# Splitting the last weight panels of two attention cores by columns instead of by contraction halves

## The reference

```python
def chunk_attention(u, w_in, b_in, rel_bias, w_out):
    q, k, v = jnp.split(u @ w_in + b_in, 3, axis=-1)
    ...
    s = jnp.einsum('bhtd,bhjd->bhtj', qi, kb).astype(jnp.float32) + bias
    p = jax.nn.softmax(jnp.where(mb, s, NEG_INF), axis=-1).astype(vb.dtype)
    return jnp.einsum('bhtj,bhjd->bhtd', p, vb)

def odd_mixer(h, w_in, b_f, qnorm_g, knorm_g, w_out):
    q, k, v, g, fl = jnp.split(proj, ...)
```

## Time and profile before

| what | value |
|---|---|
| median of 3 runs | 1955.74 us |
| the profiled execution's own time | 1954.02 us |
| its span | 1952.3 us |
| TensorE busy | 1828.4 us, 94% |
| VectorE / ScalarE / POOL busy | 1202.0 / 754.5 / 799.3 us |
| mean granted TensorE clock | 0.964 |
| first attention core, from its first scores | 756.1 to 917.6 us |
| second attention core | 1740.9 to 1904.1 us |

### The profile page before, as it was taken

How to read it: one execution, slowest core, us unless ns; L and a number is a source line. 1 busy time by engine, 2 the same in 40 slices (tenths; PEclk the granted TensorE clock), 3 DMA queues, 4 the chain that set the end, 5 groups by cost and what they waited for, 6 DMA issues and landing times.

```text
span 1952.3 us, 24973 instructions
## 1 busy us (share of the span) xinstructions
PE 1828.4 (94%) x9107; PEld 1475.1 (76%) x9107; DVE 1202.0 (62%) x1783; ACT 754.5 (39%) x1180; POOL 799.3 (41%) x577
## 2 busy tenths in 40 slices
PE   4997999999999999989999999998999999999989
PEld 3775687788888777767778888886788777777767
DVE  5786456976677942654587777687388733125562
ACT  3333335222222333544432222325335545554450
POOL 4432335556556443222446556552423343432222
PEclk8998999999999999988999999998999999999899
DMA  8543325455554232221266455541211222322211
GB/s 329 194 151 114 124 87 183 151 159 178 175 170 146 93 114 85 68 73 66 65 200 203 154 172 164 172 140 52 78 65 59 77 67 68 105 89 74 66 55 44
DMA packets 116905, 235.70 MB, mean 121 GB/s; under 512 B 8113, under 2 KB 25393, under 8 KB 115793
## 3 DMA queue, kind: packets, MB, share of 16 engines
q1 hardware_dynamic: 113776, 227.17, 35.5%
q10 hardware_dynamic: 3040, 7.34, 1.1%
HBM read 232.36 MB, written 2.13 MB: 120 GB/s over the span
## 4 chain that ended last, share of the span: by engine, by line
PE 40%; issue 34%; POOL 20%; DVE 4%; ACT 2%; POOLq 0%; DVEq 0%; ACTq 0%
PE bank L216 20%; POOL wsp L2189 19%; PE bank L429 9%; PE bank L1272 2%; PE bank L1313 2%; PE bank L1276 1%; PE bank L1383 1%; PE bank L1367 1%; PE bank L1344 1%; PE bank L1771 1%; PE bank L1548 1%; ACT wsp L179 0%; PE bank L313 0%; PE bank L619 0%; DVE fP L1445 0%
## 5 line engine op out<-in xcount | busy, mean ns | idle before, releaser
L2189 POOL TENSOR_TENSOR wsp<-raw,wsp 128x512 fp32r<-128x512 f32 x528 | 786.3, 1520 | 1133.0 <-ACT wsp L179 1133.0
L216 PE MATMUL bank<-xT,wsp 128*128 128x512 f32 x2592 | 606.9, 394 | 5.2 <-POOL wsp L2189 3.6
L216 PEld LDWEIGHTS bank<-xT,wsp 128*128 128x128 f32 x2592 | 487.7, 189 | 116.0 <-issue 7.5
L179 ACT ACTIVATE wsp<-raw 128x2048 fp32r<-128x2048 f32 x132 | 252.0, 1913 | 576.1 <-PE bank L429 248.4
L429 PE MATMUL bank<-wsp,hT 128*128 128x512 f32 x1344 | 322.0, 400 | 10.4 <-POOL wsp L2189 8.3
L216 PE MATMUL bank<-wsp,xT 128*128 128x512 f32 x1248 | 305.1, 400 | 17.7 <-DVE gg L1148 9.8
L429 PEld LDWEIGHTS bank<-wsp,hT 128*128 128x128 f32 x1344 | 255.5, 191 | 74.9 <-issue 9.0
L216 PEld LDWEIGHTS bank<-wsp,xT 128*128 128x128 f32 x1248 | 234.8, 191 | 75.5 <-DVE gg L1148 10.5
L530 DVE TENSOR_TENSOR h<-h 128x512 f32<-128x512 f32 x64 | 57.2, 909 | 79.9 <-ACT h L487 79.6
L547 DVE TENSOR_TENSOR htmp<-bank,gate 128x512 f32<-128x512 f32 x112 | 76.8, 686 | 47.8 <-PE bank L429 47.8
L1272 PE MATMUL bank<-xT,wsp 128*128 128x512 f32 x384 | 100.2, 411 | 0.3 <-DVE gT L1688 0.3
(11 more groups left out here) (304 smaller groups left out, 2133.8 us busy)
## 6 DMA issues: line engine op xcount, KB each, us to landing
raw<-in_ff_w SPq DMA_DIRECT2D x64, 1024.0 KB, 5.5
ada_ring<-in_w_ada SPq DMA_DIRECT2D x48, 384.0 KB, 3.6
ada_ring<-in_ada_w SPq DMA_DIRECT2D x48, 384.0 KB, 3.7
ring<-in_w_ada SPq DMA_DIRECT2D x64, 256.0 KB, 3.2
raw<-in_odd_w_in SPq DMA_DIRECT2D x16, 1024.0 KB, 5.5
raw<-in_gla_w_in SPq DMA_DIRECT2D x12, 1024.0 KB, 5.9
raw<-in_att_w_in SPq DMA_DIRECT2D x12, 1024.0 KB, 5.1
raw<-in_even_w_in SPq DMA_DIRECT2D x12, 1024.0 KB, 5.1
```

Source lines behind the costliest of these rows:

```text
L179: act.activation(wsp[:, slot, 0], raw[:, slot], ACT.Copy).then_inc(hi_made, 1)
L216: mm = pe.matmul(out_ap, l, r, start=(start and n == 0), stop=(stop and n == 2))
L2189: ins = pool.tensor_tensor(wsp[:, slot, 1, k], raw[:, slot, k], wsp[:, slot, 0, k].bitcast(F32), ALU.subtract)
```

## The change

The three panels inside each core become six column halves: 256 columns over the whole contraction, 1 MB each, half number `half` in slot `half % 2`. `by_columns` views a slot as 8 k tiles of 256 columns. `sp_column_half` loads one, in runs of 256 floats. A column half holds two T tiles of 128 rows of the result, or four N tiles of 256 columns. A T tile is cut along k into pieces of 4 + 4 (`TWO`), 3 + 3 + 2 (`THREE`) or 2 + 2 + 2 + 2 k (`FOUR`), one for each unit; an N tile stays in one unit. The units are consecutive: the first core has pieces in units 0 to 26, the second in 0 to 31. In the second core the values, four tiles of 512 columns before, become eight of 256. The last tile of a half releases one slot; the iteration's eviction comes ahead of that slot's copy. The order of columns, of `bank_free` numbers and of gate tiles follows (in the second core: gates 0 to 3, values of pairs 4 and 5, gates 4 and 5, values of pairs 6 and 7, gates 6 and 7). SP's order around it is the same, with six loads for six in each core.

```diff
-                tiles += 22 if n == "att_in" else 3 * c
+                tiles += 3 * PHASE0[n] + 10 if n in PHASE0 else 3 * c
...
+        def by_columns(half):
+            return half.rearrange("p k (two n) -> p (k two) n", two=2)
+        def sp_column_half(sp, name, half, at):
+            j = base[name] + 2 * PHASE0[name] + half
+            sp.wait_ge(lo_made, j - 1)
+            sp.dma_start(by_columns(raw[:, half % 2]), W[name][:, :, at:at + COLS // 2]).then_inc(raw_ld[half % 2], 16)
...
+        def in_slots(halves):
+            out, u, n, done = {}, 0, 0, 0
+            for half, tiles in enumerate(halves):
+                for i, (kind, at, cuts) in enumerate(tiles):
                     last = i == len(tiles) - 1
-                    if tile[0] == "N" and tile[3] == COLS // 2:
-                        out[u] = [(seq, i, k, tile, 0, last), (seq, i, k, tile, 1, last)]
+                    done += not last
+                    for k0, k1 in zip((0, *cuts), (*cuts, KT)):
+                        out[u] = (half, i, n, kind, at, k0, k1, last, done)
                         u += 1
+                    n += 1
...
+        TWO, THREE, FOUR = (4,), (3, 6), (2, 4, 6)
+        def turned_tiles(p, *cuts):
+            return [("T", (p, i), c) for i, c in enumerate(cuts)]
+        VALUES = [("N", t, ()) for t in range(ST)]
+        ATT_IN = in_slots([turned_tiles(4, THREE, TWO), turned_tiles(5, THREE, TWO), VALUES,
+                           turned_tiles(6, THREE, TWO), turned_tiles(7, TWO, TWO), VALUES])
+        ODD_IN = in_slots([turned_tiles(0, THREE, THREE), turned_tiles(2, TWO, THREE), VALUES,
+                           turned_tiles(4, THREE, TWO), VALUES, turned_tiles(6, FOUR, FOUR)])
...
+        def gate_number(p):
+            return p if p < 4 else p + 4 if p < 6 else p + 8
...
+        def wait_slot_tile(eng, name, piece):
+            half, last, done = piece[0], piece[7], piece[8]
+            if last:
+                eng.wait_ge(w_used, base[name] + 2 * PHASE0[name] + half + 1)
+            else:
+                eng.wait_ge(tile_done, tile0[name] + 3 * PHASE0[name] + done)
...
+        def pe_slot_piece(pe, name, ts, piece):
+            half, i, number, kind, _, k0, k1, last, _ = piece
+            if k0 == 0:
+                pe.wait_ge(TS[ts]["bank_free"], KT + ST * PHASE0[name] + number)
+            for k in range(k0, k1):
+                if i == 0 and k % 2 == 0:
+                    low_ready(pe, base[name] + 2 * PHASE0[name] + half, k // 2)
+                for n, (a, b) in enumerate(PASSES):
+                    start, stop = k == 0 and n == 0, k == KT - 1 and n == 2
+                    w = by_columns(wsp[:, half % 2, b])[:, k]
+                    if kind == "T":
+                        mm = pe.matmul(bank[D_BANK][:, :], w[:, i * P:i * P + P], xT[:, a, k, :], start=start, stop=stop)
...
-        T4 = [("T", i) for i in range(4)]
-        ATT_IN = in_slots([(0, 3, T4), (10, 4, [("T", 0), ("T", 1)] + [("N", t, COLS // 2, COLS // 2) for t in range(ST)]),
-                           (20, 5, [("T", 0), ("T", 1)] + [("N", t, COLS // 2, COLS // 2) for t in range(ST)])])
-        ODD_IN = in_slots([(0, 5, T4), (10, 6, [("N", t, 0, COLS) for t in range(ST)]), (20, 7, T4)])
...
-        def wait_slot_tile(eng, name, seq, i, last):
-            if last:
-                eng.wait_ge(w_used, base[name] + 2 * seq + 2)
-            else:
-                eng.wait_ge(tile_done, panel_tile(name, seq, i))
...
+                        mm = pe.matmul(bank[D_BANK][:, 0:COLS // 2], xT[:, a, k, i * P:i * P + P], w, start=start, stop=stop)
+            if k1 == KT:
+                mm.then_inc(w_used if last else tile_done, 1)
...
-                for piece in work.get(u, []):
-                    pe_slot_piece(pe, name, ts, piece)
+                if u in work:
+                    pe_slot_piece(pe, name, ts, work[u])
...
-            if name == "att_in":
-                before = 6 if p < 6 else 12
-            else:
-                before = 4
+            before = 4 if p < 6 else {"att_in": 12, "odd_in": 10}[name]
...
-                for seq, i, k, tile, h, last in now:
+                if u in work and work[u][6] == KT:
+                    half, _, _, kind, at, _, _, last, _ = work[u]
+                    wait_slot_tile(act, name, work[u])
+                    evac(half, kind, at)
                     if last:
-                        act_high(act, base[name] // 2 + seq + 1, h)
-                for seq, i, k, tile, h, last in now:
-                    if h == 1:
-                        wait_slot_tile(act, name, seq, i, last)
-                        evac(seq, i, tile)
+                        act_high(act, base[name] // 2 + PHASE0[name] + half // 2 + 1, half % 2)
...
+            def evac(half, kind, at):
+                if kind == "T":
+                    p, i = at
+                    (query, key)[i](p, bank[D_BANK][:, :]).then_inc(free, 1)
                 else:
-                    c = COLS + (seq - 4) * (COLS // 2)
-                    act.activation(tok[:, tile[1], c:c + COLS // 2], bank[D_BANK][:, 0:COLS // 2], ACT.Copy).then_inc(free, 1)
+                    c = COLS if half == 2 else COLS + COLS // 2
+                    act.activation(tok[:, at, c:c + COLS // 2], bank[D_BANK][:, 0:COLS // 2], ACT.Copy).then_inc(free, 1)
...
-            tile_of = {4: (0, 1), 5: (2, 3), 6: (4, 5), 7: (10, 11)}
+            tile_of = {4: (0, 1), 5: (2, 3), 6: (8, 9), 7: (10, 11)}
...
+            def evac(half, kind, at):
+                if kind == "N":
+                    c = COLS if half == 2 else COLS + COLS // 2
+                    act.activation(tok[:, at, c:c + COLS // 2], bank[D_BANK][:, 0:COLS // 2], ACT.Copy).then_inc(free, 1)
                 else:
-                    if seq == 7:
-                        act.wait_ge(s["ol"], PAIRS + i + 1)
-                    act.activation(gT[:, i], bank[D_BANK][:, :], ACT.Tanh, scale=0.5).then_inc(s["z"], 1)
+                    p = sum(at)
+                    if p >= ST:
+                        act.wait_ge(s["ol"], PAIRS + p - ST + 1)
+                    act.activation(gT[:, p % ST], bank[D_BANK][:, :], ACT.Tanh, scale=0.5).then_inc(s["z"], 1)
...
+                if u in ODD_IN and ODD_IN[u][3] == "T" and ODD_IN[u][6] == KT:
+                    p = sum(ODD_IN[u][4])
+                    dve.wait_ge(s["z"], p + 2)
+                    dve.scalar_tensor_tensor(gT[:, p % ST], gT[:, p % ST], 1.0, bank[D_BANK][:, :], ALU.add, ALU.mult)\
+                        .then_inc(free, 1)
...
-                    dve.wait_ge(free, KT + 5 * ST + (p + 1 if p < ST else ST + p + 1))
+                    dve.wait_ge(free, KT + 5 * ST + gate_number(p) + 1)
...
-            sp_panels(sp, "att_in", 6)
+            sp_panels(sp, "att_in", PHASE0["att_in"])
+            for half in range(6):
+                sp_column_half(sp, "att_in", half, PHASE0["att_in"] * COLS + half * (COLS // 2))
             sp_panels(sp, "att_out", 2)
...
-            for seq, panel in enumerate((0, 2, 1, 3, 4, 6, 5, 7)):
+            for seq, panel in enumerate((0, 2, 1, 3, 4)):
                 for h in range(2):
                     sp_half(sp, base["odd_in"] + 2 * seq + h, h, W["odd_in"][:, HK * h:HK * h + HK, panel * COLS:panel * COLS + COLS])
                 if seq == 3:
                     fox_sp_bias(sp)
+            for half, panel in enumerate((6, 6.5, 5, 7, 5.5, 7.5)):
+                sp_column_half(sp, "odd_in", half, int(panel * COLS))
             sp_panels(sp, "odd_out", 2)
...
-    order = [q[0:4], k[0:4], v[0:4], q[4], k[4], q[5], k[5], q[6], k[6], v[4:6], q[7], k[7], v[6:8]]
+    order = [q[0:4], k[0:4], v[0:4], q[4], k[4], q[5], k[5], v[4:6], q[6], k[6], q[7], k[7], v[6:8]]
```

More of the change, by code:

```diff
@@ new lines, in in_slots @@
+            return out
+        TWO, THREE, FOUR = (4,), (3, 6), (2, 4, 6)
[6 more added lines that the diff above has]
+                           turned_tiles(4, THREE, TWO), VALUES, turned_tiles(6, FOUR, FOUR)])
@@ L1398, in act_pairs @@
             for u in range(NU + 4):
-                now = work.get(u, [])
                 if u >= 6 and u % ST == high_at:
@@ L1632, in fox_act @@
             act.preload_act_table_set("exp_and_others")
-            def evac(seq, i, tile):
-                if tile[0] == "N":
-                    act.activation(tok[:, tile[1], COLS:D], bank[D_BANK][:, :], ACT.Copy).then_inc(free, 1)
-                else:
-                    if seq == 7:
-                        act.wait_ge(s["ol"], PAIRS + i + 1)
-                    act.activation(gT[:, i], bank[D_BANK][:, :], ACT.Tanh, scale=0.5).then_inc(s["z"], 1)
+            def evac(half, kind, at):
+                if kind == "N":
+                    c = COLS if half == 2 else COLS + COLS // 2
+                    act.activation(tok[:, at, c:c + COLS // 2], bank[D_BANK][:, 0:COLS // 2], ACT.Copy).then_inc(free, 1)
+                else:
+                    p = sum(at)
+                    if p >= ST:
```

(8 more changed lines are left out.)

## The result

The changed kernel takes 1936.85 us (median of 4 runs, 1933.62 to 1939.97) against 1956.40 us for the kernel before beside it: ratio 0.9899, 95% interval 0.9883 to 0.9914, so 19.6 us less. The forecast was 1941.0 with a range of 1929 to 1951; the likeliest case, 1936 to 1947, holds it.

A forecast was written before the change was run, and what follows sets the result against it. TensorE, busy 94% of the span, left idle or low-clock time to win: holes 28.4 us, tails 16.9. Terms -28.4 + 0.9 + 1.6 + 15.2 + 1.0 - 5.1 = -14.8 us gave 1941.0, range 1929 to 1951.

The forecast's parts named there:

- the likeliest case: Whole kernel: the prediction's own forecast, 1936 to 1947 us, chance 0.55.
- Holes filled: Units without pieces in the middle of both cores: their 28.4 us go if new pieces are ready and hide as much.
- PE work: Second core's four 512-column value tiles become eight of 256: +0.9 us; first core 0.
- Loads and slot conversions: 1 KB load runs, landing in 5.1 to 21 us, and slots ready 7.2 us after their last tile: 0.
- rival D: Pieces not ready (1 KB runs, or slot copy queued behind exp), PE stands at low parts: 1956 to 1965; chance 0.04.
- Short pieces: Bare 2-k pieces at 512-wide units (7 first core, 27 and 31 second) cost about 0.5 us each: +1.6 us.
- VectorE against POOL: VectorE's scalings and splits delayed by POOL's low parts beside filled units: +15.2 us, bounds 0 and 40.
- the low clock behind such waits: Lower PE clock after long waits: 1.5 us at unit 15 of the first core, 1.5 at unit 11 of the second.
- Tails: Bare units at each core's end: first core +1.0 us, second core -5.1 us (3.5 lost instead of 8.6).
- A: Better: slack takes nearly all of the VectorE and POOL contention, 4 instead of 15.2: -26, 1930 us; chance 0.2.
- B: Small gain: contention costs 26, not 15.2: -3, so 1953 us (1948 to 1955); chance 0.15.
- C: Slower: VectorE's scaling and splits beside POOL's low parts cost more than 30 us; at 36, 1962 us; chance 0.06.

The follow-up runs named there:

- POOL's low parts thin: Changed kernel with low parts of the twelve slots converted inside the cores cut from 512 to 32 columns, the rest left out: 1928.2 us, ratio 0.9864.
- the dense runs: Two kernels with column halves and consecutive 4-k pieces, against the kernel before: units 0 to 23, 1934.3 us; units 3 to 26, 1952.6 us.
- the offset run: Column halves with consecutive 4-k pieces, every piece three units later (units 3 to 26 instead of 0 to 23): 1952.6 us, 0.9980 of the kernel before.
- dense 4-k kernel: Changed kernel with every 512-column tile in two 4-k pieces, consecutive in units 0 to 23 of both cores: 1934.3 us, 0.9891 of the kernel before.
- the kernel with holes kept: Column halves, but 4-k pieces only at the units where pieces stood before, so holes stay bare: 1948.4 us, 0.9965 of the kernel before.

## Why the prediction was right, and where its terms were off

Direction, range and likeliest case hold, and the mechanism is shown: PE had no piece in the holes, and the gain is where the holes were. The sum, -14.8 against -19.6 measured (-22.1 by the cores), is 5 to 7 us short. By its own steps, and with its own measure, from start to start: a wait in brackets is less than the time lost by it, since a piece without a wait behind it lasts some 0.16 us longer than it holds up the next row. (826.86 to 830.05 in the changed kernel, a 3-k piece in front of a wait of 0.85 us, is 3.19 instead of 2.19, so 1.00 lost.)

- **Holes filled, -28.4.** No wait over 1 us is left in units 8, 9, 18 and 19 of either core. Right.
- **PE work, +0.9.** Right as far as it went, but it left out that a cut costs something itself. Two pieces of the changed kernel, start to start, 763.65 to 765.84 in the first core for 3 k and 1753.53 to 1755.03 in the second for 2 k, give 2.19 and 1.50 us, so 5.88 for 3 + 3 + 2 against 5.72 for 4 + 4, and 6.0 for four pieces. Seven tiles of the one kind and two of the other: 1.7 us that were not in the sum.
- **Loads and slot conversions, 0.** 5.1 to 5.2 us to land, at the lower bound of 5.1 to 21. Inside the first core no matmul waits for a low part, in the second PE's only such wait is 0.2 us of a weight load. Right, and rival D is out.
- **Short pieces, +1.6.** The waits at 2-k pieces in front of 512-wide units are 0.32 (unit 7), 0.32 and 0.30 us, which is 0.48, 0.47 and 0.47 from start to start: the 0.5 each was right. But there are two that I had at nothing, 0.29 and 0.28 us (0.44 lost each) at the 2-k piece of unit 2 in either core, beside a 384-wide unit.
- **VectorE against POOL, +15.2.** The step that was mis-sized. All waits of PE beside pieces, this term and the one before together, are 3.1 us in the first core and 5.5 in the second by the brackets, 8.6; from start to start 4.1 and 7.3, so 11.4 against 16.8. With POOL's low parts thin, 0.9 and 2.3 of that are left, so VectorE against POOL is some 8 us. Where I had taken a conversion beside a 512-wide unit (15, 19, 23 in the first core; 15 in the second) there is a wait, 0.85, 0.85, 0.77 and 1.07 us (1.00, 1.02, 0.92 and 1.22 lost; I had 2.0, 0.65, 0.65 and 1.4 without the clock). The 3 us for the low clock behind such waits do not exist. The PE timeline of the second core at its worst wait, and the next:

```profile
1780.68 0.44 PE L1385 MATMUL bank<-fPT,tok 128*64 128x128 f32 x4 [0.59 <-DVE gT L1693]
...
1785.62 0.88 PE L1369 MATMUL bank<-ident,fP 128*128 128x128 f32 x6 [1.44 <-DVE fP L1442]
...
1806.75 0.87 PE L1369 MATMUL bank<-ident,fP 128*128 128x128 f32 x6 [1.07 <-DVE fP L1442]
```

  The VectorE operations that I named for unit 11 (gate product, output product, split) do stand in a row ahead of its reduces. They cost 0.59 us before its piece, which stays with POOL's low parts thin, and the scalings 1.44 behind it (0.65 and 1.60 lost), instead of 2.5 + 1.5; six transposes behind it take 0.88 us, the full clock. Units 5 and 6 of the first core, which I had at 1.2, show no wait (0.26 lost in unit 6), although VectorE is held up there by POOL's block of 780.98 to 786.76:

```profile
781.12 1.52 DVE L1324 CAST aqr<-aq 128x512 fp32r<-128x512 f32 x1
782.68 1.66 DVE L1325 TENSOR_TENSOR aqr<-aq,aqr 128x512 fp32r<-128x512 f32 x1
784.26 0.54 DVE L1434 CUSTOM_DVE_ANT_0 aP<-bank,abt 128x384 f32<-128x384 f32 x1
```

  The cast takes 0.42 alone and the subtraction 0.69, but the 3-k pieces cover nearly all of it. Unit 11 of the first core (0.65) has no wait either, unit 6 of the second 0.23 instead of 1.3. The lesson of the dense runs is behind these: I charged each conversion by the width of the unit alone, where its phase to VectorE's scalings decides.
- **Tails, +1.0 and -5.1.** By the same count as in the prediction, from unit 27's start (886.69) to 910.96 the first core takes 24.27 us, less 10.0, 3.0 and 3.6 for the modulation matmuls: 7.7 lost, so -0.6 instead of +1.0. One conversion less is worth more than one bare unit costs. The second core, from unit 31's piece: 1883.74 - 1875.66 = 8.08, less 1.43, 2.18 - 0.9 and 3.0: 2.4 lost, -6.2 instead of -5.1.

Corrected, the sum is -28.4 + 0.9 + 1.7 + 10.9 - 0.6 - 6.2 = -21.7, where 10.9 is the 11.4 less the 0.5 of unit 31's piece, which the second core's tail already has. That is 0.4 us from the cores' 22.1, and the modulation matmuls, which the tails leave out, took 0.4 less (3.63 for 4.02). With the bracketed waits, 8.6, it would be 2 us too much.

Of the rivals, A (the slack takes nearly all of the contention, 4 us left, -26) is half right: the 8 us lie between its 4 and my 15.2. B is out. C, slower, needed 30 us of contention; with POOL nearly gone the changed kernel gains 9 to 10. But the offset run shows that it was no empty case: the same halves, dense and put three units later, with three bare units at the start, give back all but 4 us of the gain.

## What to carry to other kernels

When a piece of work hides a loop on another engine, look first at which stretches have no such piece, and whether the resource that it waits for can be freed in smaller parts; freeing alone gave 1 to 6 us a core here, freeing and filling 9 to 13. Then look at when the helper engine's block (here POOL's) meets the loop: in the first core the same block was free in one unit of four and cost 0.6 to 0.9 us in another. A schedule that always ends its buffers at the right unit and has more filled units was 10 us faster by the medians, 6 by the cores; filling more units with other cuts alone was 6 and 3. Gather what must stay bare at the end rather than in the middle. And when waits are added up to explain a loss, take them from start to start: the idle time in brackets missed a quarter of it here.

## What was not expected of the hardware

- Two scalings of VectorE that take 0.75 us alone take 2.67 when POOL's block starts 0.2 us ahead of them, and those that start ahead of the block keep their time (0.88 for two 512-wide ones). It is the order of starting that matters. One by one, the two held-up scalings take 1.32 and 1.43 us, each about as long as one of POOL's subtractions there (1.28 to 1.39). The Trainium skill, SBUF — State Buffer, "Who interferes with whom", says of VectorE instructions in a two-port mode that whoever issues first holds the shared ports for the whole instruction and the other is fully blocked; these rows agree.
- Not all of VectorE's work is held up. The reduce that reads a PSUM bank takes 0.54 us in the middle of POOL's block (the row at 784.26 above) and 0.56 without POOL, while the cast and the subtraction just before it take two to four times their time.
- After the same wait of 2.54 us at its start, the first core began at the low clock in one profile and at the full one in another. The first piece of the changed kernel (nine matmuls) and of the dense 4-k kernel (twelve):

```profile
759.35 3.82 PE L1279 MATMUL bank<-xT,wsp 128*128 128x512 f32 x9
```

```profile
763.00 3.01 PE L1279 MATMUL bank<-xT,wsp 128*128 128x512 f32 x12
```

  3.82 us for nine, 3.01 for twelve. The tail has the same scatter (32 modulation matmuls in 3.63 to 5.07 us), and the second core's first piece too, behind a wait of 2.59 us. What decides it stays open; it moves a core by 1.5 to 3 us.
- Single waits of up to 1.44 us in an otherwise busy stretch did not bring the clock down in the second core of the changed kernel (mean 1.00), while two waits of 1.24 and 1.54 us close together did in the second core of the kernel with holes kept.
